# Recurrence of a two-direction gated encoder: lower bound of the gates as a relu on ScalarE, first products copied by ScalarE

## The reference, cut to the recurrence

```python
def forget_gates(z, lb):
    f = lb + (1.0 - lb) * jax.nn.sigmoid(z)
    log_f = jnp.log(jnp.maximum(f, F_MIN))          # F_MIN = 1e-30
    k = (1.0 - lb) * jax.nn.sigmoid(-z)
    return k, log_f

    # per chunk: b = cumsum(log_f), S = state
    o_inter = einsum(qc * exp(b), S)
    a = einsum('bhtk,bhsk,bhtsk->bhts', qc, kc, exp(b_t - b_s))   # s <= t
    o = o_inter + einsum(a, vc)
    S = exp(b_last)[..., None] * S + einsum(kc * exp(b_last - b), vc)
```

## Time and profile before

| | us |
|---|---|
| median of three runs | 2776.69 (2776.19 to 2777.66) |
| the profiled execution, own time | 2781.77 |
| its span on the core | 2780.0 |
| PE busy in the span | 2676.1 (96%) |
| DVE busy | 1824.2 (66%) |
| ACT busy | 1412.7 (51%) |
| POOL busy | 564.4 (20%) |

### The profile page before, as it was taken

The page is one execution under the profiler, slowest core; times in us unless marked ns, Lnnn a source line. Parts: engine busy times, 40 slices in busy tenths (PEclk is TensorE's granted clock), DMA queues, the critical chain, the costliest instruction groups (busy, mean ns, idle before and its releaser), DMA issues.

```text
span 2780.0 us, 44757 instructions
## 1 busy us (share of the span) xinstructions
PE 2676.1 (96%) x18308; PEld 2148.3 (77%) x18308; DVE 1824.2 (66%) x2299; ACT 1412.7 (51%) x1783; POOL 564.4 (20%) x488
## 2 busy tenths in 40 slices
PE   9999999999999999994999999999999999999997
PEld 7888888878888778872777777777777777777775
DVE  7212232778999666566767767766776776677788
ACT  3112222867664433322656655665665666566674
POOL 2000030005554333320001100110001110111435
PEclk9999999999999999996999999999999999999999
DMA  7478876776465653426778787887887788778983
GB/s 246 167 209 243 268 241 152 158 280 229 162 222 199 219 198 117 140 81 243 287 277 306 284 305 278 303 291 277 298 310 286 278 294 316 286 288 322 362 325 129
DMA packets 237452, 686.26 MB, mean 247 GB/s; under 512 B 18729, under 2 KB 65208, under 8 KB 232128
## 3 DMA queue, kind: packets, MB, share of 16 engines
q1 hardware_dynamic: 220480, 630.58, 63.7%
q0 software_dynamic: 16768, 52.82, 7.1%
HBM read 577.46 MB, written 105.88 MB: 246 GB/s over the span
## 4 chain that ended last, share of the span: by engine, by line
PE 49%; DVE 1%; DMA 1%; POOL 1%; issue 1%; ACT 0%; ACTq 0%; DVEq 0%; POOLq 0%
PE moe_strip L2561 12%; PE moe_up L2576 4%; PE moe_gate L2576 4%; PE moe_gate L2578 4%; PE moe_up L2577 4%; PE moe_gate L2577 4%; PE moe_up L2578 4%; PE moe_down L2576 4%; PE moe_down L2577 4%; PE moe_down L2578 4%; DMA out<-moe_norm_x 1%; DVE pieces_low L2769 1%; PE moe_up L2502 1%; PE moe_turn L2536 0%; PE moe_gate L2511 0%
## 5 line engine op out<-in xcount | busy, mean ns | idle before, releaser
L2769 DVE TENSOR_TENSOR pieces_low<-pieces_raw,moe_high 128x1024 fp32r<-128x1024 f32 x768 | 893.0, 1217 | 355.5 <-PE moe_strip L2561 345.8
L2661 ACT ACTIVATE moe_high<-pieces_raw 128x1024 fp32r<-128x1024 f32 x768 | 769.6, 1052 | 361.5 <-PE moe_up L2578 195.7
L2561 PE MATMUL moe_strip<-pieces_raw,moe_xT_p 128*32 128x256 f32 x4096 | 230.4, 383 | 1.0 <-ACT moe_xT_p L2673 1.0
L2561 PEld LDWEIGHTS moe_strip<-pieces_raw,moe_xT_p 128*32 128x32 f32 x4096 | 130.5, 111 | 96.8 <-issue 14.0
L2576 PE MATMUL moe_gate<-moe_high,moe_xT 128*128 128x512 f32 x512 | 202.3, 395 | 1.9 <-DVE pieces_low L2769 1.7
L2576 PE MATMUL moe_up<-moe_high,moe_xT 128*128 128x512 f32 x512 | 203.0, 396 | 0.2 <-issue 0.2
L2576 PE MATMUL moe_down<-moe_high,moe_hdn 128*128 128x512 f32 x512 | 202.5, 396 | 0.0
L2578 PE MATMUL moe_gate<-pieces_low,moe_xT 128*128 128x512 f32 x512 | 199.7, 390 | 0.0
L2577 PE MATMUL moe_up<-moe_high,moe_xT 128*128 128x512 f32 x512 | 199.6, 390 | 0.0
L2577 PE MATMUL moe_down<-moe_high,moe_hdn 128*128 128x512 f32 x512 | 199.5, 390 | 0.0
L2577 PE MATMUL moe_gate<-moe_high,moe_xT 128*128 128x512 f32 x512 | 199.5, 390 | 0.0
(11 more groups left out here) (375 smaller groups left out, 5707.2 us busy)
## 6 DMA issues: line engine op xcount, KB each, us to landing
pieces_raw<-in_w_gate_e SPq DMA_DIRECT2D x128, 1024.0 KB, 6.0
pieces_raw<-in_w_up_e SPq DMA_DIRECT2D x128, 1024.0 KB, 8.8
pieces_raw<-in_w_down_e SPq DMA_DIRECT2D x128, 1024.0 KB, 4.9
bias_fx<-xs SPq DMA_DIRECT2D x40, 1024.0 KB, 5.4
fr_raw<-in_w_in SPq DMA_DIRECT2D x16, 1024.0 KB, 9.2
ws<-fr_late_split SPq DMA_DIRECT2D x32, 512.0 KB, 4.6
bias_fw<-ws SPq DMA_DIRECT2D x32, 512.0 KB, 7.7
mo_gates<-h SPq DMA_DIRECT2D x20, 512.0 KB, 4.3
```

Source lines behind the costliest of these rows:

```text
L2561: last = nc.tensor.matmul(strip_ps[j * CP:(j + 1) * CP, kind, :], x, raw[g % RAW][:, k * D + j * STRIP:k * D + (j + 1) * STRIP], start=sta ...
L2661: nc.scalar.activation(high[:, g % HI, cols], raw[g % RAW][:, cols], ACT.Copy).then_inc(hi_done, 1)
L2769: nc.vector.tensor_tensor(low[g % RAW][:, cols], raw[g % RAW][:, cols], high[:, g % HI, cols].bitcast(F32), ALU.subtract).then_inc(lo_done, 1)
```

## The change

1. For heads 1 to 3, ACT makes `lf` itself: Relu(s*(1-lb) + (lb - 2^-60)), one more ACTIVATE per direction ahead of the Identity (new L1202). L1308 on DVE falls away for them. The logarithm of `lf` gets 2^-60 as its bias, which gives max(f, 2^-60) again.
2. For head 0, DVE keeps its instruction, which now subtracts 2^-60 after the maximum. Two small constants are made at the stage's start (a 128x8 subtraction and a memset of one column).
3. Product 0 is taken out of PSUM by ACT: three plain copies per head (`open_pairs`, new L1235 to L1242), between `exp(hd, 2)` and `copy_keys(hd, 1)`. `gather(0)` on DVE falls away; ACT now waits for `o_stored` there. What the copies bring besides the diagonal is overwritten by the masked levels.
4. `a_done` counts 7 levels instead of 8, and a new `a_opened` counts ACT's copies; PE and DVE wait for it at level 1.

```diff
@@ pairs (PE)
-                            before = (hd * NL + n - 1) * NG + g + 1
-                            if before > 0:
-                                pe.wait_ge(a_done, before)
+                            if n == 1:
+                                pe.wait_ge(a_opened, hd * NG + g + 1)
+                            elif hd + n > 0:
+                                pe.wait_ge(a_done, (hd * LEVELS + max(n - 1, 0) - 1) * NG + g + 1)
@@ gates (ACT)
-                        one_less, least = (x[:, d, p:p + 1] for x in (omlb, lb))
+                        one_less, least, over = (x[:, d, p:p + 1] for x in (omlb, lb, lb_over))
                         act.wait_ge(z_opened, (p - 1) * 2 + d + 1)
+                        nc.scalar.activation(lf[:, d], f[:, d], ACT.Relu, bias=over, scale=one_less)
                         nc.scalar.activation(f[:, d], f[:, d], ACT.Identity, bias=least, scale=one_less)
@@ logarithms (ACT)
-                        nc.scalar.activation(lf[:, d], lf[:, d], ACT.Ln)
+                        nc.scalar.activation(lf[:, d], lf[:, d], ACT.Ln, bias=split[:])
@@ new, called by head (ACT) in round 2 ahead of copy_keys(hd, 1)
+                def open_pairs(hd):
+
+                    if hd >= 1:
+                        act.wait_ge(o_stored, 16 * hd)
+                    for g, (a, count) in enumerate(CHUNK_GROUPS):
+                        act.wait_ge(l_mm, hd * NL * NG + g + 1)
+                        nc.scalar.activation(A[:, a * P:(a + count) * P], l_ps[g][:, 0:count * P], ACT.Copy)\
+                          .then_inc(a_opened, 1)
@@ clamp (DVE); prepare_first keeps its own maximum
-                    nc.vector.tensor_scalar(lf[:, d], f[:, d], LN_SPLIT, None, ALU.max).then_inc(chain, 1)
-                    dve.wait_ge(chain, count)
                     nc.vector.tensor_scalar(f[:, d], f[:, d], F_MIN, LN_SPLIT, ALU.max, ALU.min).then_inc(clamped, 1)
@@ gather (DVE)
-                            if n == 0:
-                                if hd >= 1:
-                                    dve.wait_ge(o_stored, 16 * hd)
-                                nc.vector.tensor_tensor(chunked(A[:, cols]), chunked(l_ps[g][:, 0:width]),
-                                                        ident[:].unsqueeze(1).to_broadcast([P, count, P]), ALU.mult)\
-                                  .then_inc(a_done, 1)
@@ head (DVE)
-                    gather(0)
```

More of the change, by code:

```diff
@@ L887, in stage_recurrence @@
     MASKS = 1 + 2 * LEVELS
-    SETUP, PER = 5 + 3 + MASKS, 3 * 2
+    SETUP, PER = 5 + 2 + 3 + MASKS, 3 * 2
     U = len(LATER) * NT
@@ L907, in stage_recurrence @@
         below = W[:, 0, 1, 512:1024]
-        omlb = s.sb("omlb", [P, 2, HG_HEADS])
+        omlb, lb_over = s.sb("omlb", [P, 2, HG_HEADS]), s.sb("lb_over", [P, 2, HG_HEADS])
+        split = s.sb("split", [P, 1])
         lb_e, lb_r = s.sb("lb_e", [P, 2, HG_HEADS]), s.sb("lb_r", [P, 2, HG_HEADS])
@@ L920, in stage_recurrence @@
              "a_done", "ds_mm", "s_made", "o_mm", "o_copied", "chain", "lb_ready"))
-        z_opened = s.sem("z_opened")
+        z_opened, a_opened = s.sem("z_opened"), s.sem("a_opened")
         ki_groups = [(0, a, n) for a, n in CHUNK_GROUPS] + [(1, a, n) for a, n in reversed(CHUNK_GROUPS)]
@@ L1153, in head @@
                             fill((hd, "pairs", n))
-                    pe.wait_ge(a_done, (hd + 1) * NL * NG)
+                    pe.wait_ge(a_done, (hd + 1) * LEVELS * NG)
                     pe.wait_ge(s_made, (hd + 1) * NS)
@@ L1246, in head @@
                         if r == 2:
+                            open_pairs(hd)
                             copy_keys(hd, 1)
@@ L1283, in _ @@
                 step.next()
+                nc.vector.tensor_scalar(lb_over[:], lb[:], LN_SPLIT, None, ALU.subtract).then_inc(chain, 1)
+                step.next()
+                nc.vector.memset(split[:], LN_SPLIT).then_inc(chain, 1)
+                step.next()
                 for d in range(2):
@@ L1304, in masks, with clamp @@
                         dve.wait_ge(chain, step.next())
-                def clamp(d, count):
-                    nc.vector.tensor_scalar(lf[:, d], f[:, d], LN_SPLIT, None, ALU.max).then_inc(chain, 1)
-                    dve.wait_ge(chain, count)
+                def clamp(d):
                     nc.vector.tensor_scalar(f[:, d], f[:, d], F_MIN, LN_SPLIT, ALU.max, ALU.min).then_inc(clamped, 1)
@@ L1322, in prepare_first @@
                         dve.wait_ge(chain, count_of.next())
-                        clamp(d, count_of.next())
+                        nc.vector.tensor_scalar(lf[:, d], f[:, d], LN_SPLIT, LN_SPLIT, ALU.max, ALU.subtract)\
+                          .then_inc(chain, 1)
+                        dve.wait_ge(chain, count_of.next())
+                        clamp(d)
                 def prepare(p, d):
                     dve.wait_ge(z_done, p * 2 + d + 1)
-                    clamp(d, SETUP + PER + (p - 1) * 2 + d + 1)
+                    clamp(d)
                 def run_sums(p):
@@ L1364, in gather @@
                             dve.wait_ge(l_mm, (hd * NL + n) * NG + g + 1)
-                            if n == 0:
-                                if hd >= 1:
-                                    dve.wait_ge(o_stored, 16 * hd)
-                                nc.vector.tensor_tensor(chunked(A[:, cols]), chunked(l_ps[g][:, 0:width]),
-                                                        ident[:].unsqueeze(1).to_broadcast([P, count, P]), ALU.mult)\
-                                  .then_inc(a_done, 1)
-                            else:
-                                dve.wait_ge(a_done, (hd * NL + n - 1) * NG + g + 1)
-                                nc.vector.copy_predicated(A[:, cols], mask[:, n - 1, 0:width], l_ps[g][:, 0:width])\
-                                  .then_inc(a_done, 1)
+                            if n == 1:
+                                dve.wait_ge(a_opened, hd * NG + g + 1)
+                            else:
+                                dve.wait_ge(a_done, (hd * LEVELS + n - 2) * NG + g + 1)
+                            nc.vector.copy_predicated(A[:, cols], mask[:, n - 1, 0:width], l_ps[g][:, 0:width])\
+                              .then_inc(a_done, 1)
                     def states():
```

## The result

| | before | after |
|---|---|---|
| median | 2777.66 us (2776.19 to 2779.54) | 2791.31 us (2789.42 to 2793.61) |
| ratio | | 1.0049 (95% interval 1.0038 to 1.0060) |
| profiled execution, own time / span | 2781.77 / 2780.0 us | 2789.42 / 2787.6 us |
| first matmul of the filler to ACT's last copy in the recurrence | 596.21 to 951.17: 354.96 us | 595.99 to 964.06: 368.07 us |

The account below looks back on a forecast made before the run. PE is busy 96% of the span, but in the recurrence PE and DVE both run nearly full; heads +2.7 + 1.5 + 0.8 - 1.2 = +3.8, plus clock 2.4, gave +6.2 us: 2782.9 us, range 2775.9 to 2787.8.

Parts of the forecast that it names:

- PE's first two waits: PE's new waits for ACT's late filler evictions: 4.9 us in head 0, 2.5 in head 1.
- POOL's price: DVE's moved-up SBUF work meets POOL, whose third piece releases `exp(0, 3)`: 0 to 1 us, taken as 0.5.
- without the clock: Sum over the four heads before any loss to a lower PE clock: +3.8 us.
- Net +2.7: Head 0: PE resumes 3.2 us later after the eviction, less 0.49 of slack: +2.7 us (2.2 to 3.4).
- DVE is late by less than PE: Head 0: `exp(0, 4)` ends at 665.8, 1.8 us after DVE needs it, less one removed L1308, so PE decides.
- round 4 was to start 1.5 us late: Head 1: exponential 2.3 us later, less one L1308 of 0.81; DVE decides: +1.5 us (0.5 to 2.5).
- Half of three at 1.6 is 2.4 us: Clock falls behind half of PE's three new waits, 1.6 us lost each: +2.4 us.
- Further on it has 0.49 us of slack: Head 0: a later PE wait of 0.49 us for a gather would absorb part of the eviction's delay.
- Head 2: Eviction margin 0.40 us, a new PE wait of 2.8, slack 2.01: +0.8 us (0 to 2).
- Head 3: No gates; the gather is gone and PE's 1.53 us wait for a state can be had: -1.2 us (-1.5 to 0).
- DVE paces the head: Rival: DVE's relief passes through at levels 3 to 6, -6 to -12 us, about 2768; chance 0.05.
- ACT's room: Rival: ACT, busy 52 of 81 us, absorbs the added work; gains and costs cancel, 0, 2776.7 us; chance 0.12.

Follow-up runs that it names:

- after_warm_again: Repeat on one shared chip: changed kernel with small identity transposes on PE in its three waits for an eviction; 2785.98 us, ratio 1.0041, stage 361.19 us.
- before_early: Kernel before, with the first of the two evictions behind the gates moved up to just after the sigmoids; ratio 0.9998, stage 354.64 us.
- after_again: Changed kernel run again unaltered, as common base on one chip; 2791.09 us, ratio 1.0053 to the kernel before, stage 366.14 us.
- after_early: Changed kernel with the first eviction behind the gates moved up between the sigmoids and the Relus; ratio 1.0002, stage 355.28 us; repeated: 1.0006, 356.91 us.
- copies_early: Kernel before plus only ACT's copies of product 0, DVE's maximum kept, and the first eviction moved up behind the sigmoids; ratio 1.0000, stage 353.71 us.
- copies_only: Kernel before plus only ACT's copies of product 0; the gates' maximum stays on DVE; ratio 0.9995, stage 352.55 us.
- after_warm: Changed kernel with 50, 20 and 44 identity transposes on PE in its three waits for an eviction, first run; ratio 1.0050, stage 361.04 us.
- relu_none: Changed kernel without the Relus and without a DVE maximum in heads 1 to 3; ratio 1.0018, stage 356.85 us; repeated: 1.0011, 357.12 us.

## Why the direction was right and the size was not

Confirmed by rows: the place and the order of the mechanism, the Relu's 1.35 us (forecast 1.35), PE's first two waits (5.72 and 2.38 against 4.9 and 2.5), no wait of PE for a state in heads 0 to 2, no cost of the copies by themselves. "The bias of the logarithm is an operand, and costs nothing either" was nearly so: the logarithm with it has a median of 1.36 us instead of 1.27. POOL's price, taken as 0.5, was larger: `exp(0, 3)` starts 1.07 us later, counted from the stage's start (642.64 against 641.79), 1.29 in the second profile and 1.71 in `after_warm_again`. Part of this is scatter between profiles, for in `before_early`, with DVE's and POOL's work as before, it starts 0.53 later.

The increments of the stage by head, from sums to sums; the warm kernel is the nearest to the forecast's "without the clock". It has one fall fewer than before, so the row behind its falls adds 1.6 us where before has a fall that it lacks, and takes 1.6 off where it has one that before lacks (sums are of the unrounded numbers):

| | head 0 | head 1 | head 2 | head 3 | sum |
|---|---|---|---|---|---|
| forecast, without the clock | +2.7 | +1.5 | +0.8 | -1.2 | +3.8 |
| changed kernel | +6.9 | +2.9 | +3.0 | +0.3 | +13.1 |
| its second profile, `after_again` | +5.0 | +2.6 | +3.5 | +0.1 | +11.2 |
| falls, in both (before has 0, 2, 1, 0) | 1 | 2 | 1 | 1 | |
| `after_warm_again` | +4.4 | +0.9 | +1.2 | -0.4 | +6.2 |
| its falls | 0 | 1 | 0 | 1 | |
| the same at before's number of falls | +4.4 | +2.5 | +2.8 | -2.0 | +7.8 |
| `after_early`, which has no loss | +2.6 | -1.3 | -0.2 | -0.7 | +0.3 |

One profile stands behind each row, and that of before has the shortest head 0 of all fourteen (99.13 us; `before_early`, `copies_early` and `copies_only`, none of them slower, have 100.53, 100.10 and 101.30 and regain it later). Of what is said on head 0, 1 to 2 us can be scatter.

**The step that failed first** is head 0's, "Net +2.7", on both of its sides. PE's side: the half behind the eviction was to come 3.2 us late; from the stage's start it comes 3.8 us late in the changed kernel, 4.0 in its second profile and 4.4 in the warm one. The Relus' share is as forecast, the surplus is that of `exp(0, 3)` above. DVE's side: "DVE: ... now 665.8, 1.8 late, less one L1308: DVE is late by less than PE". Round 4 did start about as late as that (666.17, 2.4 us later from the stage's start). But the first L1308 stood ahead of an idle time of DVE, so its removal only made the wait longer (4.46 us), and the second one was offset in the warm kernel by slower rows: 3.05 us late at round 4 plus 1.39 for the longer stretch are the 4.4 at its sums. In `after_early` a part did come off, 3.0 late at round 4 and 2.6 at the sums.

In head 1 round 4 was to start 1.5 us late. Counted from head 0's sums it starts 0.1 late (49.66 us against 49.58), and the 2.9 us arise behind it, where DVE waits 4.42 us for `exp(1, 6)`; in the warm kernel it waits 1.70 there and the head takes 0.9 more. Over the stage the waits were thus worth 6.2 us as measured, or 7.8 at before's number of falls, in place of 3.8. The 7.8 is an estimate, and a fall need not reach the end in full: `before_early` has one fall in its heads where before has three, and a stage only 0.3 us shorter.

**The second** is the clock's: "Half of three at 1.6 is 2.4 us". The size of one fall was nearly right (1.6 to 2.2 in the changed kernel's first profile, but more behind the 4.36 us, where the first product alone took 4.61 us instead of 2.47), the number was not: all three new waits brought a fall where half were counted, and measured they are worth 3 to 5 us instead of 2.4. The wait of 4.36 us for DVE brought one too, as the one of 1.99 there had before. More important, the forecast gave a fall its own 1.6 us, and followed the late eviction only to `exp(hd, 4)`. The unit behind the wait is itself evicted ahead of `exp(hd, 5)`. In the changed kernel 3.8 us of a late start and 2.0 of slow matmuls met there and made `exp(0, 5)` 5.8 us later from the stage's start; DVE then waited 1.68, 0.15 and 0.64 us for PE up to its sums. That is about the 2.4 us by which head 0 exceeds the warm kernel's. In the second profile these waits are 1.05 and 0.15 us and head 0 exceeds the warm one's by 0.6, so the size of this return is uncertain; in head 1 the wait for `exp(1, 6)` shows it in both profiles. "Further on it has 0.49 us of slack" was true and of no help.

**Head 2** was sized from a PE that arrives as before (a wait of 2.8); from head 1's sums PE came 1.9 us sooner than before (the fall at 788 us was gone), the eviction 3.5 us later, and it waited 5.19. **Head 3**: the wait of 1.53 for a state was gained, as forecast, and a fall of the clock behind the wait of 2.27 us ahead of head 2's outputs, which lie in this piece, took it back (at 881.56; before had none behind 2.29).

As for the rivals: behind round 4 of head 0 DVE has no idle time in the warm kernel and PE one wait of 0.15 us, so DVE paces the head there as much as PE, more than the forecast allowed, but for the loss and not for a gain; ACT's room of 52 us in 81 covered nothing. What stays open: the clock's share finer than 3 to 5 us of 14 (the first profile of `after_warm` would give 7.0 by the stage), whether the copies cost something beside the Relus, why `relu_none` is slower than before, and why the changed kernel's stage differs by 1.9 us between its two profiles (368.07 and 366.14), 1.8 of it in head 0.

## What to carry to other kernels

In a hand-ordered list, ask of an instruction not how full its engine is but what stands behind it, and follow a delayed eviction round the whole loop: to the engine that waits for the bank, to the unit that this engine then finishes late, and to what stands behind that unit's eviction. Work taken from an engine ahead of an idle time only makes that idle time longer: compare the stretches behind it, with and without the work. When a short instruction releases a waiting engine, put it ahead of the long ones: one 0.58 us eviction moved up was worth 13 us here.

## What was not expected of the hardware

- The same DVE instructions, with no idle time between them, took 30.94, 30.97, 32.45 and 32.72 us without the maximum, and 31.31, 31.33, 32.18 and 33.13 with it. Single rows in them differ more: a subtraction 0.81 or 1.91 us, a product 1.48 or 2.64. POOL worked beside the slow ones of `after_warm_again`. Taking out 1.59 us can vanish in that.
- A wait of the same length is followed by a lower clock at one time and not at another: in the changed kernel 2.27 and 2.38 us were, 2.31 us (at 712.10) was not; in before 1.99, 2.30 and 2.31 were, 2.01 and 2.29 were not. The three waits over 4 us all were, and the clock fell in them already, at 659.7 in the first, which ended at 662.15.
- Transposes of the identity in two waits (5.6 and 5.0 us of them) kept the granted clock of both stretches at 1.00, where it had been 0.79 and 0.61.
- A logarithm with a bias from an SBUF column took 1.36 us instead of 1.27 (128x1280, float32), and a Relu with scale and bias 1.44.
